# Loads, convolution, rotation and last store of a two-layer fp32 kernel cut into smaller pieces

## The reference

```python
# layer 1: gated linear attention (4 heads) beside dilated attention (8 heads), then a gated feed-forward net
h = rms_norm(x, norm1_g);  proj = h @ w_in
x = x + concat(gla(...), dilated(...)) @ w_out
h2 = rms_norm(x, norm2_g); x = x + (silu(h2 @ w_gate) * (h2 @ w_up)) @ w_down
# layer 2 (even): retention (4 heads) beside a gated causal convolution of width 3
q, k, v, g_ret, gate_b, gate_c, u, g_conv = split(rms_norm_2(x) @ ev_w_in, 8)
conv_out = gate_b * conv3(gate_c * u) * silu(g_conv)
x = x + concat(rms_norm_nogain(retention(rope(q), rope(k), v)) * silu(g_ret), conv_out) @ ev_w_out
# layer 3 (odd): attention in a window of 128 with sinks, 32 query heads of 64, 4 key heads
q, k, v, gate = split(rms_norm_2(x) @ od_w_in)
q = rope(rms_norm_2(q, q_norm_w)); k = rope(rms_norm_2(k, k_norm_w))
x = x + (swa_sinks(q, k, v) * silu(gate)) @ od_w_out
```

## Time and profile before

| | us |
|---|---|
| median of 3 runs | 1961.87 (1960.36 to 1962.66) |
| the profiled execution, its own time | 1960.36 |
| its span, first to last instruction | 1958.6 |
| PE busy | 1941.1 (99% of the span) |
| PE weight loads busy (beside the matmuls) | 1597.7 (82%) |
| DVE busy | 1134.5 (58%) |
| ACT busy | 932.0 (48%) |
| POOL busy | 14.8 (1%) |

### The profile page before, as it was taken

The page is one execution under the profiler, slowest core; times in us unless marked ns, Lnnn a source line. Parts: engine busy times, 40 slices in busy tenths (PEclk is TensorE's granted clock), DMA queues, the critical chain, the costliest instruction groups (busy, mean ns, idle before and its releaser), DMA issues.

```text
span 1958.6 us, 22542 instructions
## 1 busy us (share of the span) xinstructions
PE 1941.1 (99%) x9023; PEld 1597.7 (82%) x9023; DVE 1134.5 (58%) x1563; ACT 932.0 (48%) x1231; POOL 14.8 (1%) x33
## 2 busy tenths in 40 slices
PE   8999999999999999999999999999999999999998
PEld 7888887888888888888888888888788888777787
DVE  5655466765445444554445566545655667677764
ACT  6545454554443344443444554444444455655553
POOL 0001000000000000000000000000000000000000
PEclk9999999999999999999999999999999999999999
DMA  8666664566665666656666566665566556554444
GB/s 295 196 189 148 179 179 136 173 182 192 188 189 191 195 187 191 192 187 193 193 190 190 184 188 184 196 193 169 150 192 190 189 180 184 151 149 140 143 147 162
DMA packets 182968, 354.86 MB, mean 181 GB/s; under 512 B 11248, under 2 KB 11568, under 8 KB 182864
## 3 DMA queue, kind: packets, MB, share of 16 engines
q1 hardware_dynamic: 181728, 350.78, 59.2%
q0 software_dynamic: 848, 2.12, 0.9%
q10 hardware_dynamic: 288, 0.52, 0.1%
HBM read 351.27 MB, written 2.11 MB: 180 GB/s over the span
## 4 chain that ended last, share of the span: by engine, by line
PE 96%; DVE 3%; issue 0%; ACT 0%; DMA 0%; DVEq 0%; ACTq 0%; POOLq 0%
PE g L829 30%; PE g L831 30%; PE g L830 30%; PE m L791 2%; DVE TW L1282 1%; DVE wl L1282 1%; PE m L909 1%; PE ob L927 0%; PE ob L926 0%; PE m L901 0%; PE ob L925 0%; PE m L899 0%; DVE st L1285 0%; DMA small<-in_small 0%; PE m L991 0%
## 5 line engine op out<-in xcount | busy, mean ns | idle before, releaser
L1282 DVE TENSOR_TENSOR wl<-raw,wh 128x1024 fp32r<-128x1024 f32 (+1 forms) x657 | 802.2, 1222 | 714.3 <-ACT wh L1032 713.2
L1032 ACT ACTIVATE wh<-raw 128x1024 fp32r<-128x1024 f32 (+1 forms) x658 | 695.3, 1057 | 793.1 <-PE g L831 790.9
L829 PE MATMUL g<-wh,xh 128*128 128x512 f32 x1888 | 748.6, 397 | 6.6 <-DVE xl L1285 3.6
L831 PE MATMUL g<-wh,xl 128*128 128x512 f32 x1888 | 737.1, 390 | 0.0
L830 PE MATMUL g<-wl,xh 128*128 128x512 f32 x1888 | 736.0, 390 | 0.0
L829 PEld LDWEIGHTS g<-wh,xh 128*128 128x128 f32 x1888 | 355.2, 188 | 83.0 <-issue 9.5
L831 PEld LDWEIGHTS g<-wh,xl 128*128 128x128 f32 x1888 | 355.0, 188 | 75.5
L830 PEld LDWEIGHTS g<-wl,xh 128*128 128x128 f32 x1888 | 355.6, 188 | 70.7
L829 PE MATMUL g<-wh,mh 128*128 128x512 f32 x736 | 291.4, 396 | 0.0
L831 PE MATMUL g<-wh,ml 128*128 128x512 f32 x736 | 287.0, 390 | 0.0
L830 PE MATMUL g<-wl,mh 128*128 128x512 f32 x736 | 286.6, 389 | 0.0
(11 more groups left out here) (132 smaller groups left out, 771.0 us busy)
## 6 DMA issues: line engine op xcount, KB each, us to landing
raw<-in_ev_w_in SPq DMA_DIRECT2D x128, 512.0 KB, 3.8
raw<-in_w_in SPq DMA_DIRECT2D x95, 512.0 KB, 4.2
raw<-in_w_gate SPq DMA_DIRECT2D x88, 512.0 KB, 4.4
raw<-in_w_up SPq DMA_DIRECT2D x88, 512.0 KB, 3.8
raw<-in_w_down SPq DMA_DIRECT2D x88, 512.0 KB, 4.8
raw<-in_od_w_in SPq DMA_DIRECT2D x72, 512.0 KB, 3.7
raw<-in_w_out SPq DMA_DIRECT2D x32, 512.0 KB, 4.5
raw<-in_ev_w_out SPq DMA_DIRECT2D x32, 512.0 KB, 4.6
```

The lines of the kernel that those rows point to most:

```text
L829: e.matmul(o, hi[:, kt, c], h, start=first, stop=False)
L831: last = e.matmul(o, lo[:, kt, c], h, start=False, stop=end)
L1032: return e.activation(o, i, AF.Copy, scale=scale)
L1282: return e.tensor_tensor(o, a, b, op)
```

## The change

It has four parts that touch different places. (1) xT's first part is cut in two parts of one `kt`; n1 moves from POOL's queue to SP's, second there; PE's first unit asks for the high parts alone first, then the low weights, then the low activations. (2) `conv` becomes four steps of one channel group, at steps 6, 9, 12 and 15. (3) The rotation of token half 1 moves to POOL with its own scratch, half 0 stays on DVE and both are one planner step; the norm does half 1 first; the steps become: square 1, sum 3, root 4, norm 6, rotation 7, turn 0 at 10, turn 1 at 13 (keys: dup at 11, turns at 13 and 14). (4) The last unit works through token half 0 first and announces it; the last add is in three parts, and the last store in three, one of them from ACT's queue.

```diff
-XPARTS = ((0, 2), (2, 4), (4, 8), (8, 12), (12, 16))
+XPARTS = ((0, 1), (1, 2), (2, 4), (4, 8), (8, 12), (12, 16))
+XPIECES = ((0, 1), (1, 2)) + tuple((kt, kt + 2) for kt in range(2, KT, 2))
...
-            yield 1
-            say("conv", j, 0)
-            yield 2
-            say("conv", j, 1)
+            for c in range(4):
+                yield 1 if c == 0 else 3
+                say("conv", j, c)
...
             yield from self.od_norm("k")
-            yield 2
+            yield 4
             say("ok_dup")
...
             yield from self.od_norm(a[0])
-            yield 3
             for k in range(2):
+                yield 3
                 say("oq_turn", a[0], k)
-                yield 1
...
     def od_norm(self, x):
-        for p in ("on_sq", "on_sum", "on_root", "on_norm"):
-            yield 2
+        for p, n in (("on_sq", 1), ("on_sum", 2), ("on_root", 1), ("on_norm", 2), ("on_rope", 1)):
+            yield n
             self.say(p, x)
-        for k in range(2):
-            yield 1
-            self.say("on_rope", x, k)
...
+                    if u == 0:
+                        o = [z[:, :] for z in g2(0)]
+                        h, l = wh[:, 0, 0:512], wl[:, 0, 0:512]
+                        on.wait_ge(s_hi, 1)
+                        on.wait_ge(s_split, 1)
+                        for k in range(2):
+                            e.matmul(o[k], hi[:, 0, 128 * k:128 * k + 128], h, start=True, stop=False)
+                        on.wait_ge(s_lo, 1)
+                        for k in range(2):
+                            e.matmul(o[k], hi[:, 0, 128 * k:128 * k + 128], l, start=False, stop=False)
+                        on.wait_ge(s_first, 1)
+                        for k in range(2):
+                            last = e.matmul(o[k], lo[:, 0, 128 * k:128 * k + 128], h, start=False, stop=False)
+                        last.then_inc(s_mul, 1)
+                        continue
+                    if u == N - 1:
...
+                        k, c = half, slice(128 * half, 128 * half + 128)
+                        o = g2(u)[k][:, :]
+                        for i, kt in enumerate(un.kts):
+                            h, l = (z[:, u % NS, 512 * i:512 * i + 512] for z in (wh, wl))
+                            e.matmul(o, hi[:, kt, c], h, start=False, stop=False)
+                            e.matmul(o, hi[:, kt, c], l, start=False, stop=False)
+                            last = e.matmul(o, lo[:, kt, c], h, start=False, stop=i == 1)
+                        last.then_inc(s_mul if k else s_tail, 1)
+                        continue
...
@@ DVE: the last add @@
+                        on.wait_ge(s_tail, 1)
+                        c = x[:, 0, 512 * j:512 * j + 512]
+                        tt(c, banks(b)[0][:, :], c, ALU.add).then_inc(s_added, 1)
+                        on.wait_ge(*product(b))
+                        for i in range(2):
+                            n = slice(256 * i, 256 * i + 256)
+                            c = x[:, 1, 512 * j + 256 * i:512 * j + 256 * i + 256]
+                            last = tt(c, banks(b)[1][:, n], c, ALU.add)
+                            if i == 0:
+                                last.then_inc(s_added, 1)
...
@@ DVE: rotation of half 0 (scratch W1); POOL runs the same six with rope_of(a[0], 1, PR) @@
+                elif kind == "on_rope":
+                    on.wait_ge(s_tables, 1 if a[0] == "k" else 2)
+                    on.wait_ge(s_on_norm, 2 * nth(*p))
+                    (a1, a2), t4, (c1, s1, c2, s2) = rope_of(a[0], 0, W1)
+                    tt(t4[0], a1, c1, ALU.mult)
+                    tt(t4[1], a2, s1, ALU.mult)
+                    tt(t4[2], a2, c2, ALU.mult)
+                    on.wait_ge(*steps.mark(tt(t4[3], a1, s2, ALU.mult)))
+                    tt(a1, t4[0], t4[1], ALU.subtract)
+                    tt(a2, t4[2], t4[3], ALU.add).then_inc(s_rope0, 1)
...
@@ POOL waits for the norm of its half alone @@
+                    on.wait_ge(s_on_norm, 2 * nth(*p) - 1)
...
-                    for k in range(2):
+                    for k in (1, 0):
...
@@ SP: the first loads @@
             turned_x(0)
-            turned_x(1)
-            load(2)
-            turned_x(2)
-            load(3)
-            turned_x(3)
-            load(4)
-            turned_x(4)
-            load(5)
+            e.dma_start(small[:, n0:n1], t["small"][:, n0:n1]).then_inc(s_n1, 16)
+            for i in range(1, 5):
+                turned_x(i)
+                load(i + 1)
+            turned_x(5)
...
@@ SP: the last store (ACT stores out[128:256, 1536:1792] behind s_added 2) @@
+                    if j == 3:
+                        on.wait_ge(s_added, 1)
+                        e.dma_start(out[0:128, 1536:2048], x[:, 0, 1536:2048]).then_inc(s_out, 16)
+                        on.wait_ge(*x_ready(4, 3))
+                        e.dma_start(out[128:256, 1792:2048], x[:, 1, 1792:2048]).then_inc(s_out, 16)
+                        continue
```

More of the change, by code:

```diff
@@ L132, in say @@
         self.order.append(p)
-        if p[0] in ("xsplit", "xturn", "mix", "cmix"):
+        if p[0] in ("xturn", "mix", "cmix"):
             for i in range(2):
                 self.there[(p[1], p[2] + i)] = p
+        if p[0] == "xsplit":
+            for kt in range(p[2], p[3]):
+                self.there[(p[1], kt)] = p
         if p[0] == "norm":
@@ L193, in first_acts @@
     def first_acts(self):
-        for kt in range(0, KT, 2):
-            self.say("xsplit", "X0", kt)
+        for lo, hi in XPIECES:
+            self.say("xsplit", "X0", lo, hi)
             yield 1
@@ L717, in program, with rope_of @@
                "q": A2[:, 2304:2560].rearrange("p (a k n) -> p a k n", a=4, k=2)}
+        def rope_of(x, k, scratch):
+            groups, n = 4 if x == "k" else 8, 32
+            half = groups * n
+            v = T3[:, k, 0:2 * half].rearrange("p (g e n) -> p g e n", g=groups, e=2)
+            places = [scratch[:, half * i:half * i + half].rearrange("p (g n) -> p g n", g=groups) for i in range(4)]
+            tables = [tab["k" if x == "k" else "q"][:, i, k, :].unsqueeze(1).to_broadcast([128, groups, n])
+                      for i in range(4)]
+            return (v[:, :, 0, :], v[:, :, 1, :]), places, tables
+        PR = A2[:, 2560:3584]
         def g2(u):
@@ L1274, in scalar @@
                     evacuate(so[:, j % 2, :, :], a[-1], AF.Silu)
+                elif kind == "out" and a[0] == 3:
+                    on.wait_ge(s_added, 2)
+                    e.dma_start(out[128:256, 1536:1792], x[:, 1, 1536:1792]).then_inc(s_out, 16)
         def vector(e):
@@ L1616, in vector, with cw @@
                         on.wait_ge(s_cmix, 2 * j)
-                    taps = []
-                    for c in range(2 * half, 2 * half + 2):
-                        def cw(tap):
-                            return C("cw", 3 * (4 * j + c) + tap, 3 * (4 * j + c) + tap + 1)
-                        on.wait_ge(*steps.mark(ts1(yc[:, c, :], mp[:, c, 2:258], cw(2), ALU.mult)))
-                        on.wait_ge(*steps.mark(stt(yc[:, c, :], mp[:, c, 1:257], cw(1), yc[:, c, :], ALU.mult,
-                                                   ALU.add)))
-                        last = stt(yc[:, c, :], mp[:, c, 0:256], cw(0), yc[:, c, :], ALU.mult, ALU.add)
-                    last.then_inc(s_conv, 1)
+                    def cw(tap):
+                        return C("cw", 3 * (4 * j + c) + tap, 3 * (4 * j + c) + tap + 1)
+                    on.wait_ge(*steps.mark(ts1(yc[:, c, :], mp[:, c, 2:258], cw(2), ALU.mult)))
+                    on.wait_ge(*steps.mark(stt(yc[:, c, :], mp[:, c, 1:257], cw(1), yc[:, c, :], ALU.mult, ALU.add)))
+                    stt(yc[:, c, :], mp[:, c, 0:256], cw(0), yc[:, c, :], ALU.mult, ALU.add).then_inc(s_conv, 1)
                     conv_done = (s_conv, nth(*p))
```

85 lines of the change are left out of this document (47 added, 38 removed).

## The result

The changed kernel takes 1968.4 us, the kernel before 1961.4 us (medians of six runs each on the same chip): a ratio of 1.0037, with a 95% interval from 1.0024 to 1.0050. It is 7.0 us slower, where 1958.4 was forecast, and lies 1.9 us above the range. Its profiled execution is its longest of the six, 1969.95 us with a span of 1968.2; that of before took 1960.36 with a span of 1958.6. So the two traces stand 9.6 us apart.

What follows compares the result with a forecast made beforehand. TensorE, busy 99% of the span, bounds the kernel, so only its 17.5 us idle can be won. Start -2.5, convolution -3.1, tail -0.9, rotation +3.0 sum to -3.5: 1958.4 us, range 1951.0 to 1966.5.

Steps and rivals of the forecast that it cites:

- forecast case: Odd layer's rotation: DVE keeps its turn while its next instruction is ready, POOL gets gaps; 3.0 us lost, chance 0.35.
- Alternation: Rotation in the odd layer: DVE and POOL take turns, one instruction each; +11.1 us there, 1966.5 in total, chance 0.28.
- h: Rotation: what one 256-column POOL instruction costs DVE; between 0.16 and 0.62 us, taken as 0.62.
- side sentence: Odd layer: idle time of 3.8 to 5 us may bring PE's clock down, each fall adding 1 to 3 us.
- What the odd layer would be without interference: Rotation in the odd layer: 4.4 us gained in blocks 1 to 3, 0.6 lost in block 0, 3.8 gained in sum.
- Its whole, 1951.6: Rival for the whole kernel: the engines hardly disturb each other, -10.3 us in total, 1951.6; chance 0.27.
- Start: Kernel start: norm weights land sooner on SP's queue, PE starts at 6.25 instead of 8.77; 2.5 us gained.
- hidden by the 2.6 us that the first six products take at half clock: Kernel start: Load(2), one issue (0.43 us) later, and xT's other parts, one load later, cause no wait.
- Convolution: Even layer's convolution: one quarter before the root lets PE's cut start at 1390.2; the whole stall, 3.1 us, is gained.
- Tail: Kernel end: half 0 stored during half 1's work, last store issued sooner and half as large; 0.9 us gained (0.5 to 1.2).
- AW and the keys: Odd layer: the AW stall of 0.66 us goes; four steps, 5.4 us, before the keys' copies make their rotation cost nothing.

Runs made afterwards that it cites:

- half the columns: The changed kernel, but GpSimd rotates only half of its heads (128 columns per instruction instead of 256), the others of half 1 staying unrotated: 1955.56 us, ratio 0.9972.

## Why the prediction was wrong

**The step that failed** is the forecast case's sentence "DVE keeps its turn as long as its next instruction is ready, POOL gets the gaps". The rows of the changed kernel show one each in turn, six times in each of the four query blocks, and for the keys too. Alternation was the second rival, with a chance of 0.28. Its form is right in detail: all six instructions fall between the norm and the end of the first rotation, the first turn alone is late, the second never. The prediction argued against it that a back-to-back DVE may not let go and that no row showed two changes of turn in a row; but no row showed DVE keeping its turn against a waiting GpSimd either. The rows left both rules open, and the chances of 0.35 and 0.28 leaned on nothing in them.

**h, the price of one instruction,** was taken as 0.62 between bounds of 0.16 and 0.62. It measured 0.53, and 0.26 for 128 columns. That it goes by the columns was right. The 0.56 estimated from the Trainium skill (GPSIMD Engine Reference, "3.1 Elementwise — side-by-side cycle accounting") lies nearer to it.

**The clock** was the second failure. The rival's time of 1966.5 left it out, and a side sentence had it as a possibility, at 1 to 3 us for each fall. It fell in all four blocks and cost 8.3 us in the trace (1.5 to 2.7 in a block), 7.0 by the medians of the run in which PE was kept busy: inside that estimate. With h = 0.53 the rival's own terms give 12.7 - 3.8 = 8.9 for the odd layer, and with the 7.0 of the clock 15.9, where the part alone measured 16.7. By the prediction's sum alternation alone gives +2.4 us in total at h = 0.53 (12.7 - 3.8 - 6.5), too little to be told from no change; the clock's share made it clear. Had the rival carried its side sentence in its price (4 x 2 us), its time would have been 1974.5 with h = 0.62 and 1972 with 0.53, and the range would have reached there.

**What the odd layer would be without interference** was right. The terms gave a gain of 3.8; over the odd layer the trace with half 1 on VectorE gains 3.9, and by the medians that kernel is 4.4 faster than the one without the rotation part. Its whole, 1951.6, stands against 1948.6 measured. Of the 3.0 between, 1.0 is the kernel before itself (1960.9 in those runs, 1961.9 in the ones that the prediction started from), 0.6 this term, and 1.0 start and tail together (2.8 and 1.65 in place of 2.5 and 0.9); 0.4 is less than the interval.

**Start.** -2.5 was the sum of a first product 2.5 sooner, all of it kept. It came 3.45 sooner: the norm weights were there before ScalarE asked for them, and the first weights were cast at 4.15 instead of 5.01. With the norm weights back on GpSimd's queue the first product still came at 6.38, so the queue accounts for about 1 us of it; why the weights landed sooner, no run here separates. Then the loads of the third unit were late, which the prediction had covered with "hidden by the 2.6 us that the first six products take at half clock". That cover went with the half clock: the first products ran at 1.00 (the window at 8.0, where before had 0.50). 1.8 us of stall followed, and the clock fell then. Kept, at the product of 59.76: 1.6 in this trace and 1.2 in the two others in which the clock fell at the start, 2.3 to 3.3 in those with the new start in which it held. The term of 2.5 was near by luck: a gain larger by one us, and a stall and a clock that the sum did not have.

**Convolution.** Right in mechanism: 3.1 forecast, 3.2 between the two traces. The part alone measured 4.6; that the clock may fall behind this stall too, worth 1.6, was not in the price. The cut was forecast for 1390.2 without what the start gives; it starts at 1388.56, and 1.6 later, in the time of before, is 1390.2. It is done 0.8 to 0.9 before PE asks for it, as worked out, and no later cut is late.

**Tail.** 0.9 came from the stores' issue and is there (the last store is issued 0.8 us behind the last matmul's end, as forecast). The remaining 0.75 is the term it left out: the last stores are smaller and land in 2.1 and 2.2 us instead of 2.5 and more.

**AW and the keys.** Right: the AW stall is gone, and the keys' rotation (0.26 for each of its instructions) makes no wait of note for the copies behind it.

## What to carry to other kernels

GpSimd is not a free second VectorE. Where VectorE works through a back-to-back queue of instructions with two SBUF inputs and something waits for its end, each GpSimd instruction that reads SBUF was put in front of one of them here; moving work there cost more than it took away (12.8 us, for 9 us of DVE work in four blocks). GpSimd instructions that only write cost VectorE nothing. Whether the move pays where DVE's queue has real gaps, no run here shows.

A stall on TensorE can have a second price behind it. Count the matmuls at half clock that may follow, put that in the rival's sum with its number, and look whether a stall can be shortened by an order of work (here two steps, 14 us) before an engine is changed.

A load that comes sooner is worth only what the next loads in the same queue leave of it; read on in the timeline to the first wait behind it.

## What the runs showed of the hardware

VectorE, with instructions of two SBUF inputs, and GpSimd, with instructions that read SBUF, took turns strictly, one instruction each, while both had one ready: 4 DVE products in 3.54 us and GpSimd ones of 0.90 each, in every block. The 1.71 of one GpSimd product is a full VectorE cut (about 1.2) and its own 0.5.

The clock did not go by the length of the stall alone. Stalls of 4.2 and 2.8 us brought it to 0.50 in all eight query blocks of the two traces that have them (the changed kernel and the rotation part alone). The convolution's stall of 3.0 did so in two traces (start alone, tail alone) and not in two others (before, rotation alone). At the start, stalls of 1.83, 2.3 and 2.4 did, and others of 1.7 to 2.4 did not. Nor did 2.6 in one execution with half the columns. What else decides, these runs leave open.

The fall can come when the stall is over: PE had worked again for 0.7 us in block 1 and for 1.4 behind the convolution's stall in the kernel with the tail alone. A half-speed stretch took 3 to 6 us of PE's work, cost 1.5 to 2.7 us, and ended by itself while PE worked without a break.
